# Turning mLSTM keys, values and heads on VectorE and DMA instead of TensorE

## The reference, cut to what matters

```
for each head and chunk:
    w    = exp(logd - m_tok);  s = (q k^T) * w
    num  = s @ v + inter * (q @ C);   den = sum(s) + inter * (q @ n)
    h    = num / max(|den|, floor)
    C, n = decay * C + sum_s w_last k v^T,  decay * n + sum_s w_last k
h  = h * rsqrt(mean(h * h) + EPS)            # per head
ya = (h * mlstm_norm * sigmoid(o)) @ w_proj_a
```

## Time and profile before

| | |
|---|---|
| median of 3 runs | 1900.24 us (1899.9 to 1901.29) |
| profiled execution | 1900.39 us, span 1898.6 us |
| TensorE (PE) busy | 1878.9 us, 99% of the span |
| VectorE (DVE) busy | 1348.6 us, 71% |
| ScalarE (ACT) busy | 868.6 us, 46% |
| granted TensorE clock | 0.999 of full |
| chain that ended last | PE 91%, DVE 5%, DMA 2% |

### The profile page before, as it was taken

The page is one execution under the profiler, slowest core; times in us unless marked ns, Lnnn a source line. Parts: engine busy times, 40 slices in busy tenths (PEclk is TensorE's granted clock), DMA queues, the critical chain, the costliest instruction groups (busy, mean ns, idle before and its releaser), DMA issues.

```text
span 1898.6 us, 33354 instructions
## 1 busy us (share of the span) xinstructions
PE 1878.9 (99%) x13291; PEld 1854.1 (98%) x13291; DVE 1348.6 (71%) x2082; ACT 868.6 (46%) x1629; POOL 110.3 (6%) x165
## 2 busy tenths in 40 slices
PE   9999999999999999999999999999999999999997
PEld 8999999999999999999999999999999999999997
DVE  7788998999997754784455378977777776736363
ACT  5554444444554455551122355644454444635342
POOL 0011111111111111110000000000000000000000
PEclk9999999999999999999999999999999999999999
DMA  3556576666657655558131332222222223556654
GB/s 135 162 142 153 161 187 161 164 185 172 189 173 199 194 157 155 145 157 339 45 139 45 119 108 96 81 69 84 76 81 69 79 81 109 188 204 208 209 171 160
DMA packets 126553, 272.88 MB, mean 144 GB/s; under 512 B 21820, under 2 KB 61500, under 8 KB 126400
## 3 DMA queue, kind: packets, MB, share of 16 engines
q1 hardware_dynamic: 111280, 235.16, 35.8%
q0 software_dynamic: 15120, 35.59, 10.4%
HBM read 206.97 MB, written 63.74 MB: 143 GB/s over the span
## 4 chain that ended last, share of the span: by engine, by line
PE 91%; DVE 5%; DMA 2%; issue 1%; ACT 1%; SPq 0%; POOL 0%; DVEq 0%; ACTq 0%; POOLq 0%
PE ps L1202 9%; PE ps L1204 9%; PE ps L1203 9%; PE ps L1367 8%; PE ps L1368 8%; PE ps L1369 8%; PE ps L1567 7%; PE ps L1565 7%; PE ps L1566 7%; PE ps L1587 4%; PE ps L1588 4%; PE ps L1589 4%; PE ps L1295 2%; PE ps L1292 1%; PE ps L1275 1%
## 5 line engine op out<-in xcount | busy, mean ns | idle before, releaser
L1202 PE MATMUL ps<-rx,fhi 128*128 128x368 f32 (+2 forms) x736 | 248.2, 337 | 0.4 <-ACT spl L1744 0.3
L1204 PE MATMUL ps<-rx,flo 128*128 128x368 f32 (+2 forms) x736 | 237.4, 323 | 0.0
L1203 PE MATMUL ps<-rx,fhi 128*128 128x368 f32 (+2 forms) x736 | 237.1, 322 | 0.0
L1367 PE MATMUL ps<-rx,ahi 128*128 128x304 f32 (+1 forms) x672 | 194.1, 289 | 0.9 <-DVE v L2588 0.8
L1368 PE MATMUL ps<-rx,ahi 128*128 128x304 f32 (+1 forms) x672 | 193.7, 288 | 0.0
L1369 PE MATMUL ps<-rx,alo 128*128 128x304 f32 (+1 forms) x672 | 193.6, 288 | 0.0
L1587 PE MATMUL ps<-ghi,dhi 128*128 128x384 f32 (+1 forms) x528 | 173.2, 328 | 2.3 <-DVE glo L2949 1.8
L1588 PE MATMUL ps<-glo,dhi 128*128 128x384 f32 (+1 forms) x528 | 172.3, 326 | 0.0
L1589 PE MATMUL ps<-ghi,dlo 128*128 128x384 f32 (+1 forms) x528 | 172.2, 326 | 0.0
L2942 DVE TENSOR_TENSOR dlo<-draw,dhi 128x1408 fp32r<-128x1408 f32 x48 | 77.8, 1625 | 117.4 <-ACT dhi L2154 117.3
L1202 PEld LDWEIGHTS ps<-rx,fhi 128*128 128x128 f32 x736 | 138.4, 188 | 2.5 <-ACT spl L1744 1.1
(11 more groups left out here) (367 smaller groups left out, 5723.1 us busy)
## 6 DMA issues: line engine op xcount, KB each, us to landing
draw<-wdn SPq DMA_DIRECT2D x48, 704.0 KB, 4.2
araw<-wts SPq DMA_DIRECT2D x105, 256.0 KB, 4.0
uraw<-wts SPq DMA_DIRECT2D x44, 512.0 KB, 4.4
fraw<-wts SPq DMA_DIRECT2D x27, 512.0 KB, 3.6
qkv<-scr_qkv SPq DMA_DIRECT2D x22, 544.0 KB, 8.3
scr_g<-cva SPq DMA_DIRECT2D x22, 512.0 KB, 2.6
alo<-wts POOLq DMA_DIRECT2D x42, 256.0 KB, 5.2
graw<-scr_g SPq DMA_DIRECT2D x43, 192.0 KB, 4.1
```

The lines of the kernel that those rows point to most:

```text
L1202: pe.matmul(b, hi[:, w], src[:, his[k], cols], start=(k == 0), stop=False)
L1203: pe.matmul(b, hi[:, w], src[:, los[k], cols], start=False, stop=False)
L1204: mm = pe.matmul(b, lo[:, w], src[:, his[k], cols], start=False, stop=(k == KB - 1))
L1367: pe.matmul(b, ahi[s][:, c], bhi[:, k, :], start=(fresh and k == 0), stop=False, skip_group_check=True)
```

## The change

Keys and values are no longer turned on TensorE. VectorE's transpose turns each 32x32 block within a 128x128 block; four DMAs per step then store the result so that in DRAM (`scr_t`) the blocks stand in their transposed places, and one DMA loads it back as rows of keys and values (`kvt`). Keys and values are both needed only through this path, so the load of a head brings four blocks (two of keys, two of queries) rather than six, and values come in pieces of 128 tokens (`vin`).

The head goes the same way back: VectorE transposes its 32x32 blocks, one store per step writes it, and the blocks are put in their places when they are loaded during PB, by four DMAs per block. The norm weight and the "+1, half" of the output gate move into one more ScalarE pass over each gate tile. The quotient goes out of the head norm, which shortens VectorE's small operations from five to two.

```diff
 SyncE
+ def load_values(i):                      # in the slot 3 before step i
+     if i >= 2: sp.wait_ge(turned_set, 2 * i - 3)
+     sp.dma_start(vin[i % 2], scr_qkv[h, 2:4, :, step_cols(j)] as "b p n -> p b n")
+ def store_turned(i):                     # 1 before
+     sp.wait_ge(turned_set, 2 * i + 2)
+     for a in range(4):
+         rows = slice(32 * a, 32 * a + 32)
+         sp.dma_start(scr_t[i][:, :, rows] as "k (b n) q -> n (k b) q",      # n=32
+                      turned[i % 2][rows] as "n k (b q) -> n (k b) q")        # q=32
+ def load_turned(i):                      # in the slot of step i, first of all
+     if i >= 2: sp.wait_ge(n_full, i - 1)
+     sp.wait_ge(turned_out, 64 * (i + 1))
+     sp.dma_start(kvt[i % 2][:, 0:2 * DH], scr_t[i] as "k n q -> n k q")
+ def store_head(i):                       # 4 after
+     sp.dma_start(scr_z[h, step_cols(j)][first:L], zs[i % 2][first:L, :])
-     for b in range(6):                   # load_head
+     for b in (0, 1, 4, 5):
  for k in range(KB):                      # during PB
-     sp.dma_start(fx[:, KB + k, :], scr_z[k])
+     heads = scr_z[h] as "(g q) (a n) -> a q g n"                            # q=32, n=32
+     for a in range(4):
+         sp.dma_start(fx[32 * a:32 * a + 32, KB + k, :] as "q (g n)", heads[4 * b + a])
      sp.dma_start(fx[:, k, :], scr_o[k])
 TensorE
-     for b in range(4): pe.transpose(bank(2, b * P, P), q[:, b, cols], ident)
-     rows_out(i): wait zt_set; 2 x pe.transpose(bank(3, ...), zt, ident)
-     pe.wait_ge(kv_copied, 2 * i + 2)
+     pe.wait_ge(kw_set, i + 1)            # in values(i)
 ScalarE
-     copy bank 2 -> vt;  copy bank 2 -> kw with scale;  2 x copy bank 3 -> zs
+ weighted_keys(i):                        # 1 after, ahead of scores
+     act.wait_ge(kvt_in[p], 16 * (i // 2 + 1))
+     scale kvt keys in place (128x256)
+ normed(i):                               # 2 after
+     act.activation(zt, hn, Copy, scale=sm[p][:, 2:3])
+     once per "o" tile: spl = Identity(spl, bias=mnq, scale=mnq)              # 128x1088
 VectorE
+ gate_columns: two more operations on the 9x4 floor columns (min, square)
+ turn(i):                                 # 2 before
+     if i >= 2: dve.wait_ge(turned_out, 64 * (i - 1))
+     dve.wait_ge(v_part_in[p], ...)
+     dve.transpose(turned[p][:, 2:4, :], vin[p]);  dve.transpose(turned[p][:, 0:2, :], keys)
+ rows_out(i):                             # 3 after
+     dve.transpose(zs[p], zt[p])
-     five 128x1 operations, and zt = hn * a * b
+     den*den max floor^2;  times DH*EPS plus the sum of squares
-     gated_head: (o + 1) * z
+     gated_head: o * z
```

More of the change, by code:

```diff
@@ L94 @@
 SPL_OF = {"u": (0, 2), "g": (1, 2), "k": (1, 1), "v": (0, 0), "q": (0, 0)}
-SPL_AT = [1 + sum(sum(SPL_OF[kind]) for kind, _ in PAIRS_B[:i]) for i in range(NB + 1)]
+SPL_AT = [2 + sum(sum(SPL_OF[kind]) for kind, _ in PAIRS_B[:i]) for i in range(NB + 1)]
 V0_STORES = [[1 - p + len(range(p, min(i, NB), 2)) for i in range(NB + 2)] for p in range(2)]
@@ L463, in build @@
     qkv = [Room(at_rz + s * 6 * blk)(f"qkv{s}", [P, 6, T]) for s in range(2)]
+    room = Room(at_rz + 2 * blk)
+    vin = [room(f"vin{s}", [P, 2, L]) for s in range(2)]
+    turned = [room(f"turned{s}", [P, 4, L]) for s in range(2)]
+    assert room.at <= at_rz + 4 * blk
     room = Room(at_rz + 6 * blk)
@@ L479, in build @@
     cb = [room(f"cb{s}", [P, 2, VW]) for s in range(2)]
-    vt = [room(f"vt{s}", [P, VW]) for s in range(2)]
-    kw = [room(f"kw{s}", [P, DH]) for s in range(2)]
+    kvt = [room(f"kvt{s}", [P, DH + VW]) for s in range(2)]
     wt = [room(f"wt{s}", [P, L]) for s in range(2)]
@@ L484, in build @@
     zt = [room(f"zt{s}", [P, DH]) for s in range(2)]
-    zs = [room(f"zs{s}", [P, 2, L]) for s in range(2)]
+    zs = [room(f"zs{s}", [P, DH]) for s in range(2)]
     nb = [room(f"nb{s}", [P, L]) for s in range(2)]
@@ L797, in load_first_head @@
                 sp.wait_ge(grp_done, b_at(NB - 1, 3, 1))
-                for b in range(4):
+                for b in range(2):
                     sp.dma_start(qkv[0][:, b, :], scr_qkv[0, b]).then_inc(qk_in, 16)
@@ L861, in _ @@
             for s, ((kind, k), c) in enumerate(SLOTS):
+                i = step_at(s, 0)
+                if i is not None:
+                    load_turned(i)
+                i = step_at(s, -1)
+                if i is not None:
+                    store_turned(i)
+                i = step_at(s, -3)
+                if i is not None:
+                    load_values(i)
                 i = step_at(s, 1)
@@ L925, in _ @@
                 if i is not None:
+                    store_head(i)
+                i = step_at(s, 4)
+                if i is not None:
                     h, j = STEPS[i]
[L927 to L933, removed]
                     if j == NCHUNK:
@@ L1153, in _ @@
             for s in range(2):
[L1154 removed]
+                pool.memset(kvt[s][:, 2 * DH:DH + VW], 1.0).then_inc(const_set, 1)
             pool.wait_ge(const_set, 15)
@@ L1881, in _ @@
                     a_hi(0, 5), a_hi(0, 6), a_hi(0, 2), a_hi(0, 7), a_hi(0, 4), a_minus(0, 2), a_minus(0, 4)
+                i = step_at(s, 1)
+                if i is not None:
+                    weighted_keys(i)
                 i = step_at(s, 0)
@@ L2660, in _ @@
                     gate_columns()
+                i = step_at(s, 3)
+                if i is not None:
+                    rows_out(i)
+                i = step_at(s, -2)
+                if i is not None:
+                    turn(i)
                 i = step_at(s, 0)
```

171 lines of the change are left out of this document (95 added, 76 removed).

## The result

The changed kernel takes 1951.93 us (median of 4 runs, 1950.55 to 1955.64), the kernel before 1900.07 beside it: ratio 1.0276, 95% interval 1.0258 to 1.0293. Slower was the likelier sign and the range of 1878 to 1965 holds the time, but the forecast of 1907.7 is 44 us off, and outside the likeliest case's own range of 1896 to 1925.

What follows compares the result with a forecast made beforehand. TensorE, busy for 99% of the span, was taken to bound the kernel. Terms of -23.4 (transposes), +2 (start), +16 (steps' queue) and +12.8 (PB) summed to +7.4 us, so 1907.7 us, range 1878 to 1965.

Steps and rivals of the forecast that it cites:

- TensorE, -23.4 us: In the steps: transposes leaving TensorE save 0.65 us in each of 36 steps, 23.4 us in all.
- VectorE and ScalarE, 0: In the steps: VectorE's net +0.3 us per step and ScalarE's -0.7 fit beside TensorE and cost nothing.
- Start of the steps, +2 (0 to 6): Before the steps: extra turns and the first key and value rows' store, landing and load cost 2 us.
- Price of a small packet, 18 ns (12 to 24): DMA engine time per 128 B packet, taken as 18 ns from the busy time of 256 B packets.
- rival A: The queue keeps up: packets near 12 ns, overlapping queues, slot 6.7 us, 1882.5 us in all; chance 0.25.
- Steps: the DMA queue: In the steps: engine need 7.5 us against a 6.65 us slot; slot taken as 7.1, costing 16 us (0 to 59).
- The chain "through SyncE": In the steps: load, four store issues, their landing and the next load in SyncE's order, about 6 to 7 us.
- PB, +12.8: In PB: small-packet head loads add 3.5 us per block, delaying the weights behind them; TensorE stalls 12.8 us.
- hidden by the transfers: In PB: 32 DMAs in place of 8 cost SyncE 10 us of issue, which the transfers hide.
- C: In the steps: the round trip sets the pace, packets 24 ns, slot 8.3 us, 1964 us in all; chance 0.16.
- D: In the steps: small stores cost a second access, 36 ns each, slot 9.8 us, 2005 us in all; chance 0.06.
- B: Steps clear but PB bites: 18 ns packets with overlap, 1893.6 us in all; chance 0.13.

Runs made afterwards that it cites:

- heads-only kernel: Changed kernel with keys and values turned by TensorE again, only heads by VectorE and DMA: 1893.33 us with PB's weights asked for earlier, 1903.43 in the changed order.
- the quotient alone: Keys, values and heads all turned by TensorE as before; only the head norm without the quotient, its weight folded into the gate: 1899.18 us, ratio 0.9995.
- the unread stores: Changed kernel keeping its four stores per step, but loading keys and values as they lie in memory, without waiting for the landing: 1951.86 us, steps 301.5.
- head store first: Changed kernel with the head's store moved to the front of its slot in SyncE's order: 1948.09 us, steps 299.4.
- head store gone: Changed kernel with heads turned by TensorE again, stored and loaded as before; keys and values stay with VectorE and DMA: 1939.0 us, steps 305.9.
- stores on ScalarE: Changed kernel with each step's four stores issued from ScalarE's queue instead of SyncE's: 1952.21 us, steps 305.3.
- no stores: Changed kernel without the four stores per step and VectorE's wait for them, keys and values loaded as they lie in memory: 1906.24 us, steps 255.8.

## Why the prediction was wrong

The measured time lies inside the range, but where a gain of 23.4 us and two losses were to nearly cancel (+7.4), the losses were 58.9 and 16.1 us where 16 and 12.8 were forecast. By its own steps:

- **TensorE, -23.4 us**: right. Keys, values and heads: the heads-only kernel takes 9.5 us out of the steps (forecast 36 x 0.22 = 7.9) and its busy time falls 8.1; the quotient alone is 1.5 or nothing. For keys and values the instructions are gone, but no kernel here was without the new loss, so their 15.5 us were not seen by themselves.
- **VectorE and ScalarE, 0**: right as to their work. The three transposes, on VectorE's lines, took what the row of the scaling had suggested (0.41):
```profile
L2413 DVE STREAM_TRANSPOSE zs<-zt 128x256 f32<-128x256 f32 x34 | 15.0, 441 | 52.9 <-DMA scr_z<-zs 52.9
L2403 DVE STREAM_TRANSPOSE turned<-vin 128x256 f32<-128x256 f32 x35 | 14.2, 407 | 12.8 <-DMA vin<-scr_qkv 12.8
L2406 DVE STREAM_TRANSPOSE turned<-qkv 128x256 f32<-128x256 f32 x35 | 14.1, 403 | 0.0
```
- **Start of the steps, +2 (0 to 6)**: +1.5 up to the first scores, but the term also named the first key and value rows, and these cost more. The first 27 us of the steps, before and changed:
```profile
573.00:600.00 27.00, 27.00 (x169) 26.10 (x168) 19.82 (x52) 13.42 (x34) 6.23 (x9) 1.00 0.84 229
```
```profile
573.00:600.00 27.00, 17.10 (x88) 15.44 (x89) 12.45 (x29) 6.25 (x13) 3.72 (x5) 0.87 0.75 167
```
  TensorE is idle for 9.9 us there, 8.5 of them in the wait for the first weighted keys; in three kernels with the same steps code it is idle for 7.0 to 9.8, with the longest waits elsewhere. In all of them the four stores of the second step stand for 5.7 to 9.4 us in SyncE. So the term was too small; the steps' 58.9 us hold the difference.
- **Price of a small packet, 18 ns (12 to 24)**: too high, at the low end that rival A took. In the steps the 128 B packets were busy for 12.9 ns on average. In PB, one microsecond with almost nothing but these (packets, MB, share of the engines, 914 to 915 us):
```profile
q1 hardware_dynamic: 1529, 0.20, 130.1%
```
  That is 16 us x 1.301 / 1529 = 13.6 ns busy, and one begun every 10.5 ns of an engine: they overlap. The sum of 7.5 us of engine time per slot came out all the same, 0.87 x 300.7 / 36 = 7.27, as other packets took longer beside the stores (those of 512 B 32.6 ns instead of the 29.2 without); 0.73 x 255.8 / 36 = 5.19 without them, so all that the stores add is 2.08 us of engine time per step. That it came out is in part luck.
- **Steps: the DMA queue, "I take a slot of 7.1 us ... +16 us (0 to 59)"**: this is the step that failed. The loss was 58.9 us, a slot of 8.35 us (300.7 / 36), the very end of the bound. Two things in it were wrong. The slot was set below the engines' need, as if they could be kept full throughout; their share was 0.87 on average, though 1.02 to 1.30 occur in PB. (A need of 7.27 us, a share of 0.87 and a slot of 8.35 are one measurement, and give no cause.) And the four issues were taken at 0.43 us each, from issues in a quiet queue; they took 1.02 on average and up to 9.4 for four, because an issue has to wait at times, by all appearance until packets ahead of it are worked off. (Its chain has 1.3 us for them, though 4 x 0.43 is 1.7.) SyncE stood at these issues for 143.3 us, where 36 x 4 x 0.43 are 62, and so asked late for the values, the turned tiles and the head store. The chain "through SyncE" was named, but priced as latencies, landing and load; the unread stores show that the landing costs nothing, and three kernels show that moving single waits in that order (head store first, head store gone, stores on ScalarE) wins under 4 us while the packets stay. What takes the loss away is fewer packets (16.8 us for 512 in place of 2048 per step), then fewer DMAs (12.4), or no stores (45.7). Whether the engines' backlog or a limit of SyncE's queue makes the issues long, no run separates.
- **The granted clock**: not in the sum at all. TensorE's work without the transposes took 15.2 us longer than it should in the steps and 5.1 in PB (100.9 against 95.8), over a quarter of the 75 us lost in both. It falls to the lower of its levels behind TensorE's stalls, as in PB of the changed kernel, between two waits for weights:
```profile
908.00:936.00 28.00, 23.34 (x142) 23.05 (x140) 6.46 (x9) 2.88 (x3) 0.00 (x0) 0.98 0.95 216
936.00:940.00 4.00, 3.02 (x10) 3.02 (x11) 3.32 (x5) 1.11 (x1) 0.00 (x0) 0.50 1.03 225
940.00:960.00 20.00, 14.65 (x75) 14.36 (x74) 5.83 (x7) 2.17 (x2) 0.00 (x0) 0.84 0.92 196
```
  In the second row the clock is 1.2 GHz, half of full speed, right behind a window in which TensorE was idle for 4.7 us.
- **PB, +12.8**: measured +16.1, in the place that was named. ScalarE's rows of the low-part weights (as the earlier trace rows; tiles 3 and 4 are the last two):
```profile
907.65 1.06 ACT L1651 ACTIVATE fhi<-fraw 128x1024 fp32r<-128x1024 f32 x1 [9.12 <-PE ps L1245]
934.62 1.06 ACT L1651 ACTIVATE fhi<-fraw 128x1024 fp32r<-128x1024 f32 x1 [11.27 <-DMA fraw<-wts]
954.11 1.06 ACT L1651 ACTIVATE fhi<-fraw 128x1024 fp32r<-128x1024 f32 x1 [14.32 <-DMA fraw<-wts]
```
  From 909.3 to 927.2 SyncE issued three blocks with their gate blocks, 5.95 us each; less the 1.36 us of a gate block that is 4.6 us per head block, forecast 4.9. The price behind it was another: 272 small packets at 13.4 ns are 3.6 us, and the 4352 B packets beside them took 223 ns in this PB where they took 178. SyncE stood at the four issues for 6.8, 4.3 and 4.4 us meanwhile; whether the engines or the issues set the pace is not shown. Nor is the piece's size the whole cause: with rows of 4352 B on the same 32 partitions a part of the loss stayed, 9.3 us by the stretch, 3.2 by the medians against one wide load. And "hidden by the transfers" was no argument about issues: SyncE can stand at an issue as long as the transfers ahead take.

Of the rivals, C (the round trip sets the pace, 1964) came nearest in time, and its mechanism is refuted by the unread stores; its price per packet, 24 ns, was not met either. A had the price and the overlap of the packets right, and the time wrong by 69 us: a cheap packet did not make the queue keep up. The sign set for C and D, slots of 8 us and more, came (8.35), and so did two set for the forecast, a share near 0.9 and longer waits of ScalarE for `fraw` (11.27 and 14.32 us). B's condition, steps clear, was met only by the heads-only kernels. D's small stores at 36 ns did not occur: they took 12.9 ns of an engine. The Trainium skill's "DMA: Bandwidth & Descriptors", section Specifications, has a read-modify-write below 512 B. No second access shows in this trace: a packet of 128 B was busy for less than half of the 29 ns of one of 512 B, though per byte for nearly twice as long.

Keys and values turned by VectorE and DMA cost 2.0% by themselves; the heads, turned so, won 0.4% with PB's weights asked for earlier and lost 0.1% without. The Trainium skill's "VectorE: DVE Perf Modes", section Rules for kernel authors, sends a full 128x128 turn to TensorE where PSUM is a good place for it: the runs agree for keys and values, and for the heads only with PB's weights in the changed kernel's order.

What stays open: the 14 us of the steps without stores; what holds an issue, the engines' time or a limit of SyncE's queue, and what a queue whose engine has nothing else to do would have gained; and, in PB, narrow DMAs against their number.

## What to carry to other kernels

Before giving TensorE's work to DMA, count packets, and do not take the engines' time per slot for the slot: here their mean share was 0.87, and the slot was 1.1 us longer than their time. Take an issue's length from a loaded queue, since the issuing engine stands there and all its later requests with it. Look at the first steps by themselves: TensorE was idle for 9.9 of their first 27 us here. When many waits end on late transfers, look at how long the issuing engine stands at its issues before moving waits about: exchanging the longest wait gave under 4 us here, three times. A stall of TensorE can be paid again in its clock: up to 20 us of 75 here.

## What the runs showed of the hardware

- A DMA issue can last 0.3 or over 9 us (9.39 at the load of values behind one store of 2048 packets); the DMA behind a small-packet store pays if the store itself does not (133.5 us at `vin` in 33 issues).
- Packets of 128 B were busy for 13 ns of an engine and overlapped: in a run of them a new one began every 10.5 ns of an engine, at a share of 1.30.
- 2048 packets of 128 B cost the same in one DMA or four (302.5 and 300.7 us of steps); 512 packets of 512 B cost 12.4 us less in one than in four (medians 1922.17 and 1934.52), and four on 32 partitions cost what four on 128 do (1934.56).
- With head loads of 4352 B rows into 32 partitions, four DMAs each, a full queue ran at 257 GB/s, where loads into 128 ran at 412, with packets of 278 ns instead of 171.
